# Tile loop of the first stage: the low half behind the moves, the halves' rows a step later, and a fourth half left to the projections

## What is computed

```python
def rmsnorm(x, g):
    y = x * lax.rsqrt(jnp.mean(x * x, axis=-1, keepdims=True) + 1e-6)
    return y * g

sh1, sc1, g1, sh2, sc2, g2 = split(silu(c) @ w_ada + b_ada, 6)   # per condition: prompt, sample
h = rmsnorm(x, norm_mix) * (1 + sc1) + sh1
qa, ka, va, fa, qb, kb, vb = split(h @ w_in)      # 8 forgetting heads, 8 band heads
logf = log_sigmoid(fa + b_f)                      # 8 gates per token
y = concat(head_rmsnorm(attend_a(qa, ka, va, cumsum(logf))),
           head_rmsnorm(attend_b(qb, kb, vb, rel_bias))) @ w_out
x = x + g1 * y
x = x + g2 * moe(rmsnorm(x, norm_ffn) * (1 + sc2) + sh2)          # 32 experts, 2 per token
out = rmsnorm(x, norm_final)
```

## Time and profile before

| | us |
|---|---|
| median of 3 runs | 1245.49 |
| lowest, highest | 1238.99, 1247.1 |
| time of the profiled execution | 1240.19 |
| its span | 1238.4 |
| PE busy in the span | 1100.7 (89%) |
| DVE, ACT, POOL busy | 491.6, 356.3, 366.4 |
| tile loop, first move to first projection | 34.66 to 90.00 |

### The profile page before, as it was taken

One profiled execution on the slowest core, in us unless ns is written; L12 is line 12 of the kernel. 1 busy time (PEld: TensorE's weight loads), 2 busy tenths in 40 slices (PEclk: granted clock), 3 DMA queues, 4 the chain that ended last, 5 costly groups with the idle time before them and its releaser, 6 DMA issues. The chain is left out here.

```text
span 1238.4 us, 20082 instructions
## 1 busy us (share of the span) xinstructions
PE 1100.7 (89%) x7180; PEld 767.1 (62%) x7180; DVE 491.6 (40%) x1307; ACT 356.3 (29%) x1130; POOL 366.4 (30%) x306
## 2 busy tenths in 40 slices
PE   5589999999999899999986899962999999989956
PEld 2348788888888788888875688851333333333322
DVE  0453344444444344453555267754111212111227
ACT  2643334434334334433454122210111111011102
POOL 1150633535353403113033144435222222121001
PEclk8799999999999999999999899975999999999978
DMA  9953323223141504021077511125999999999784
GB/s 382 404 196 110 96 69 108 93 64 101 62 118 34 166 1 120 14 72 45 1 221 212 188 69 69 69 103 215 398 374 373 413 414 393 406 368 422 281 306 158
DMA packets 86809, 238.63 MB, mean 193 GB/s; under 512 B 10456, under 2 KB 58024, under 8 KB 75952
## 3 DMA queue, kind: packets, MB, share of 16 engines
q1 hardware_dynamic: 68384, 132.01, 30.5%
q10 hardware_dynamic: 7344, 78.91, 15.8%
q0 software_dynamic: 10976, 26.32, 5.7%
HBM read 208.19 MB, written 38.45 MB: 199 GB/s over the span
## 5 line engine op out<-in xcount | busy, mean ns | idle before, releaser
L1987 PE MATMUL moe_gu_ps<-a_gu,moe_xT_sb 128*64 x416 | 185.1, 598 | 5.2 <-DMA b_gu<-in_w_gu 3.3
L942 PE MATMUL att_piece_ps<-hT_hi,w_hi 128*128 128x384 f32 (+1 forms) x528 | 184.4, 349 | 2.4 <-PEq L196 1.0
L1990 PE MATMUL moe_gu_ps<-b_gu,moe_xT_sb 128*64 128x512 f32 x416 | 185.1, 598 | 0.0
L942 PE MATMUL att_piece_ps<-hT_hi,w_lo 128*128 128x384 f32 (+1 forms) x528 | 172.7, 327 | 0.0
L942 PE MATMUL att_piece_ps<-hT_lo,w_hi 128*128 128x384 f32 (+1 forms) x528 | 172.5, 327 | 0.0
L1167 DVE COPY att_pT_sb<-att_pT_ps 128x512 f32<-128x512 f32 (+2 forms) x192 | 94.6, 520 | 133.4 <-PE att_pT_ps L1010 132.9
L1987 PEld LDWEIGHTS moe_gu_ps<-a_gu,moe_xT_sb 128*64 128x64 f32 x416 | 57.0, 138 | 125.7 <-issue 125.7
L1271 ACT ACTIVATE att_probs_sb<-att_probs_sb,att_nmax_sb 128x640 f32<-128x640 f32 (+5 forms) x144 | 101.4, 704 | 41.3 <-DVE att_nmax_sb L1153 40.6
L1289 ACT ACTIVATE keep_rows_all_sb<-att_o_ps,att_rden_sb 128x64 f32<-128x64 f32 x144 | 37.3, 310 | 246.8 <-PE att_o_ps L1031 246.8
L942 PEld LDWEIGHTS att_piece_ps<-hT_hi,w_hi 128*128 128x128 f32 x528 | 99.1, 188 | 11.1 <-issue 6.0
L1153 DVE CUSTOM_DVE_ANT_0 att_probs_sb<-att_s_ps,both_wide_sb 128x640 f32<-128x640 f32 (+5 forms) x144 | 95.3, 662 | 26.8 <-PE att_s_ps L998 15.0
(11 more groups left out here) (312 smaller groups left out, 1964.1 us busy)
## 6 DMA issues: line engine op xcount, KB each, us to landing
b_gu<-in_w_gu ACTq DMA_DIRECT2D x25, 2048.0 KB
b_dn<-in_w_dn ACTq DMA_DIRECT2D x25, 1024.0 KB
a_gu<-in_w_gu SPq DMA_DIRECT2D x10, 2048.0 KB
keep_rows_all_sb<-in_w_ada SPq DMA_DIRECT2D x9, 2048.0 KB, 11.2
att_w_raw_sb<-in_w_qkv SPq DMA_DIRECT2D x21, 512.0 KB, 3.7
a_dn<-in_w_dn SPq DMA_DIRECT2D x10, 1024.0 KB
w_out_parts<-keep_rows_all_sb SPq DMA_DIRECT2D x16, 512.0 KB, 4.8
in_w_ada_sb<-in_w_ada SPq DMA_DIRECT2D x3, 2048.0 KB, 16.6
```

The lines of the kernel that those rows point to most:

```text
L942: ins = pe.matmul(bank[:, 0:hi - lo], w[:, kind, kc, :], x[:, kc, lo:hi], start=(m == 0), stop=(m == 3 * NC - 1))
L1987: pe.matmul(gu_ps[p % 2][LANE[0], :], xT[:, c, LANE[0]], a_gu[:, bass.ds(slot, 1), c, :].rearrange("p a n -> p (a n)"), start=(c == 0), st ...
L1990: ins = pe.matmul(gu_ps[p % 2][LANE[1], :], xT[:, c, LANE[1]], b_gu[p % 3][:, c, :], start=(c == 0), stop=(c == NC - 1))
```

## The change

In the tile loop of `modulate_in`:

- Halves in the loop: four (4 to 7, at steps 2, 3, 4 and 6) in place of five (4 to 8, at steps 2 to 6). `EARLY` is 8, so four halves (8 to 11) are done in `attention`, after pieces 1, 3, 5 and 7. `W_HOME` follows.
- ScalarE copies a half's row one step after PE forms it; PE sums its columns two steps after, in place of one.
- VectorE does `lower(t - 1)` directly behind its move, ahead of `normalise` and `mean_square`, which change places.
- PE does the gate sum last in a step, behind the columns and the gate part.
- The last gate part is done in two pieces, columns of tiles 6 and 7 (256) and of tile 8 (64), each waiting for its own tiles' low half: 32 matmuls in place of 16.
- The two stores of the filler pattern are issued after all loads of the first stage (half 9 is the last), and SyncE does not wait for them there; VectorE waits for them in `attention`, before it overwrites part of their source.
- `X_FIRST`, which was `False`, is removed with its branches.

```diff
-EARLY = HALVES - 3
+EARLY = HALVES - 4
...
+    HALF_AT = {2: 4, 3: 5, 4: 6, 6: 7}
+
     def halves_at(t):
 
-        n = FIRST + t - 2
-        return [n] if FIRST <= n < min(EARLY, HALVES - HELD) else []
...
             if n == 6:
                 sp.wait_ge(xT_ready, 3)
                 sp.dma_start(raw, a["w_qkv"][0].rearrange("b p k n -> p b k n")).then_inc(raw_ld, 16)
-                sp.wait_ge(far_set, 1)
...
-        sp.wait_ge(far_stored, 32)
+        sp.wait_ge(far_set, 1)
+        entries = k["lists"].rearrange("(p n) c -> p (n c)", p=P)
+        sp.dma_start(entries[:, 0:D], far).then_inc(k["far_stored"], 16)
...
@@ scalar
-            for n in halves_at(t):
+            for n in halves_at(t - 1):
                 modulation_out(n)
...
@@ tensor, gate_part
-            pe.wait_ge(lo_done, (hi + P - 1) // P)
...
+            for n0, n1 in [(lo, min(hi, SEQ))] + [(SEQ, hi)] * (hi > SEQ):
+                pe.wait_ge(lo_done, (n1 + P - 1) // P)
+                for i, part in enumerate((h_hi, h_lo)):
+                    for kc in range(NC):
+                        ins = pe.matmul(f_ps[0:16, n0 - lo:n1 - lo], w_f_parts[:, kc, :], part[:, kc, n0:n1],
+                                        start=(i == 0 and kc == 0), stop=(i == 1 and kc == NC - 1))
...
@@ tensor, loop
-            if chunk_ending(t - 1) is not None:
-                gate_sum(chunk_ending(t - 1))
-            for n in halves_at(t - 1):
+            for n in halves_at(t - 2):
                 summed_columns(n)
             if chunk_ending(t) is not None:
                 gate_part(chunk_ending(t))
+            if chunk_ending(t - 1) is not None:
+                gate_sum(chunk_ending(t - 1))
...
@@ vector, loop
             move(t)
-            if t + ready < TILES:
-                if t + ready + 1 < TILES:
-                    mean_square(t + ready + 1)
-                normalise(t + ready)
             if t:
                 lower(t - 1)
+            if t + AHEAD < TILES:
+                normalise(t + AHEAD)
+            if t + AHEAD + 1 < TILES:
+                mean_square(t + AHEAD + 1)
...
@@ vector, attention, unit 0, step 1
                     if n == 0:
+                        dve.wait_ge(k["far_stored"], 32)
                         dve.wait_ge(pT_ready, turn["gates"] + 1)
```

More of the change, by code:

```diff
@@ L252, in modulate_in @@
     AHEAD = 3
-    X_FIRST = False
     w_ada = [k["rows_all"][:, 4 * j:4 * j + 4, :].rearrange("p t (a n) -> p (t a) n", a=2) for j in range(2)]
@@ L286, in modulate_in @@
     FIRST = 4
+    HALF_AT = {2: 4, 3: 5, 4: 6, 6: 7}
     def halves_at(t):
-        n = FIRST + t - 2
-        return [n] if FIRST <= n < min(EARLY, HALVES - HELD) else []
-    IN_LOOP = sum(len(halves_at(t)) for t in range(TILES))
+        return [HALF_AT[t]] if t in HALF_AT else []
     def chunk_ending(t):
@@ L325, in _ @@
             load_half(n)
-            if n == HELD and not X_FIRST:
+            if n == HELD:
                 for t in range(3, TILES):
@@ L404, in gate_rows_out @@
             act.activation(f_parts[:, 0:hi - lo], f_ps[:, 0:hi - lo], ACT.Copy).then_inc(f_moved, 1)
-        if X_FIRST:
-            for t in range(TILES):
-                square(t)
-            for n in range(FIRST):
-                modulation_out(n)
-        else:
-            for n in range(FIRST - 1):
-                modulation_out(n)
-            for t in range(AHEAD):
-                square(t)
-            modulation_out(FIRST - 1)
-            square(AHEAD)
+        for n in range(FIRST - 1):
+            modulation_out(n)
+        for t in range(AHEAD):
+            square(t)
+        modulation_out(FIRST - 1)
+        square(AHEAD)
         act.wait_ge(a1_done, 1)
@@ L421, in _ @@
             upper(t)
-            if t + AHEAD + 1 < TILES and not X_FIRST:
+            if t + AHEAD + 1 < TILES:
                 square(t + AHEAD + 1)
@@ L430, in _ @@
                 gate_rows_out(chunk_ending(t - 1))
-        for n in range(FIRST + IN_LOOP, EARLY):
+        for n in halves_at(TILES - 1):
             modulation_out(n)
@@ L464, in gate_part @@
             pe.wait_ge(wf_split, 2)
-            pe.wait_ge(lo_done, (hi + P - 1) // P)
             if c:
                 pe.wait_ge(z_done, c)
-            for i, part in enumerate((h_hi, h_lo)):
-                for kc in range(NC):
-                    ins = pe.matmul(f_ps[0:16, 0:hi - lo], w_f_parts[:, kc, :], part[:, kc, lo:hi],
-                                    start=(i == 0 and kc == 0), stop=(i == 1 and kc == NC - 1))
+            for n0, n1 in [(lo, min(hi, SEQ))] + [(SEQ, hi)] * (hi > SEQ):
[4 more added lines that the diff above has]
+                                        start=(i == 0 and kc == 0), stop=(i == 1 and kc == NC - 1))
             ins.then_inc(f_ready, 1)
@@ L481, in _ @@
         pe.wait_ge(silu_done, 1)
-        if X_FIRST:
-            transpose_x(0)
-            transpose_x(1)
         partial_rows(0)
         for n in range(1, FIRST):
-            if n == FIRST - 1 and not X_FIRST:
+            if n == FIRST - 1:
                 transpose_x(0)
@@ L504, in _ @@
                 gate_part(chunk_ending(t))
-        for n in halves_at(NT):
-            summed_columns(n)
-        for n in range(FIRST + IN_LOOP, EARLY):
-            partial_rows(n)
+            if chunk_ending(t - 1) is not None:
+                gate_sum(chunk_ending(t - 1))
+        for n in halves_at(TILES - 2) + halves_at(TILES - 1):
             summed_columns(n)
@@ L557, in logits @@
             dve.tensor_scalar(z[:, lo:end], f_ps[0:8, 0:end - lo], b_f[:, 0:1], None, ALU.add).then_inc(z_done, 1)
-        ready = TILES if X_FIRST else AHEAD
         mean_square(0)
-        for t in range(ready):
+        for t in range(AHEAD):
             if t + 1 < TILES:
```

30 lines of the change are left out of this document (10 added, 20 removed).

## The result

| | before | after |
|---|---|---|
| median (lowest to highest), 7 runs each | 1241.63 (1238.99 to 1247.54) | 1231.55 (1228.28 to 1234.56) |
| ratio, 95% interval | | 0.9904 (0.9881 to 0.9928) |
| profiled execution, span | 1240.19, 1238.4 | 1228.53, 1226.7 |
| first move, first projection | 34.66, 90.00 | 34.58, 73.87 |
| first transposes of probabilities, first values | 139.75, 145.04 | 126.50, 133.28 |

The change takes 10.1 us off the median; 10.4 was forecast. The same two kernels were compared twice more: 0.9923 (0.9890 to 0.9956) and 0.9933 (0.9913 to 0.9953), 9.0 us each. So the gain is 0.7 to 1.0%, small, and no comparison allows none.

A forecast was written before the change was run, and what follows sets the result against it. PE and ScalarE waiting for each other in the first stage's tile loop was taken as the bound. Stage end 90.0 to 75.5 (-14.5), +1.3 clock, +2.8 late half: net -10.4, from 1245.49 to 1235.1 us; 8 in 10 for 1230 to 1244.

The forecast's parts named there:

- the last step, where the sum is read: Reading of the whole-kernel forecast: about 1% (12.4 us) can be told from no change; within 1% given 0.66.
- the clock in the loop: Tile loop: one fall of PE's clock, 2.2 to 2.6 us, counted at half weight as 1.3 us.
- steps 1 and 2: Tile loop: later row copy cuts ScalarE's step from 6.7 to about 4.3 us; earlier low half starts tile 4's transposes about 43.65.
- step 3: Tile loop: PE becomes the longest chain, rows 1.92 us at the high clock, its list ending at 69.6 us.
- step 4: Last gate part cut in two: saves no wait, costs 3.6 us in place of about 2.5; stage ends at 75.5.
- step 5: First-stage loads: half 6 lands at 52.4 (wanted 52.5), half 7 at 61.3 (wanted 61.7); list stores cost nothing.
- third rival: Tile loop: PE stays at 1.2 GHz or a half is late; net -5 to -8 us, time 1239; chance 24%.
- step 6: Between projections: fourth late half adds 2.8 us; pair 1's V weights have 3.7 us of cover, so cost nothing.
- GpSimd last: First stage: GpSimd's three splits end at 74.6, costing nothing, or 2 us if weights land 3 us late; 1237; 10%.
- slower rival: Pair 1's V weights, behind the twelfth row and w_out in SyncE's queue, land 14 us later to break even; 3%.
- The sign: Behind the first stage: forecast wrong altogether if the stretches there change in length by more than 3 us.
- the likeliest one: Whole kernel: the forecast case, net -8 to -12.4 us, own range 1233 to 1238; chance 38%.

The follow-up runs named there:

- e3: The kernel before with only the row copy one step later and the columns two steps behind; ratio 1.0016.
- e4: The kernel before with only the low half directly behind the move; ratio 1.0009.
- e5: The kernel before with both loop edits (later row copy, low half behind the move), five halves in the loop, all else as before; ratio 1.0006.
- e2: The changed kernel with half 8 back in the tile loop at step 7, so three late halves; ratio 0.9945.
- e17: The changed kernel unaltered, compared with the kernel before a third time, on one chip with e16; ratio 0.9933.
- e1: The changed kernel unaltered, compared with the kernel before once more; ratio 0.9923.
- e9: The changed kernel with half 6 handled at step 5 in place of step 4; ratio 0.9907.
- e7: The changed kernel with the last gate part in one piece again; ratio 0.9928.
- e10: The changed kernel with spare matmuls, results never read, around the last gate part and sum and before the first transposes of probabilities; ratio 0.9869.
- e16: The same kernel as e10 run again, on one chip with the unaltered changed kernel; ratio 0.9872.

## Why the prediction came out as it did

- **What failed: the last step, where the sum is read.** "About 1% (12.4 us) is what a measurement of this kernel can tell from no change" made a forecast of -0.84% into one of no change that can be told, with 0.66 on it. The interval measured is 0.24% to either side, four times narrower, and the measured -0.96% stands clear of zero. In the sum itself three terms were off: the split gate part (3.6 against 2.5), the clock in the loop (1.3 against 0 in this profile) and the stretches behind the stage (nothing against +1.5). They and half a microsecond of PE's chain turn -10.4 into the -11.7 between the spans. That the medians differ by 10.1 is in part luck: terms of both signs, a clock that comes out differently in each execution, and a baseline of 3 runs.
- **The mutual wait, steps 1 and 2: right.** The transposes of tile 4 were put at 43.65 and stand at 43.49; ScalarE's step was put at 4.3 and is 4.0. The runs add what the prediction didn't say: neither edit alone, nor both with nothing else (e3, e4, e5), gains anything measurable; with the rest of the change, even five halves in the loop gain 0.5% (e2).
- **PE's chain, step 3: right within a microsecond.** Rows 5 to 7 ran at the high clock. The list was to end at 69.6; the last gate part starts at 69.11.
- **The split gate part, step 4: mis-sized.** Priced at 3.6 us with 1.1 for the 64-wide pieces; it took 2.5 (1.08, 1.10, 0.41, 0.40). The price came from tile 8's transposes, the upper end. The range had the lower one. With it the end of 75.5 is 74.4, measured 73.9.
- **The loads, step 5: right to 0.2 us, but its meaning was missed.** Half 6 lands at 31.75 + 20.6 = 52.4 (predicted 52.4), `raw` at 38.30 + 17.8 = 56.1 (56.2), half 7 at 48.68 + 12.4 = 61.1 (61.3). The loads of halves 6 and 7 in the trace of after:

```profile
L300 SPq DMA_DIRECT2D keep_rows_all_sb<-in_w_ada x1: 328/328/328, 31.7 to 31.7; - x1
...
DMA to landing us min/median/max: 20.6/20.6/20.6
```

```profile
L300 SPq DMA_DIRECT2D keep_rows_all_sb<-in_w_ada x1: 339/339/339, 48.7 to 48.7; - x1
...
DMA to landing us min/median/max: 12.4/12.4/12.4
```

  I treated these points as cover that might fail. They are the floor: with the mutual wait gone, half 7 lands at 60.5 to 61.9 in all profiles with this order of loads, whatever PE does, and what is left to vary is mostly the clock behind it, 12.8 to 17.5 us from the last rows to the first projection (61.1 to 73.9, 60.9 to 78.3).
- **The clock in the loop, 1.3 at half weight: mis-sized.** To the first projection it is 0 in the profiles of after and e17 and 4.5 in e1, three executions of one kernel, and 3.2 in e9. The third rival (a half late, the clock low) is therefore not another outcome but one that comes and goes between executions, with a half late (e1) or without (e9).
- **The fourth late half, step 6: right in the profile of after.** 2.88 us against 2.8; in e1 and e17 the same stretch is 4.5 longer than before (54.3 and 54.2 against 49.75), since the clock is low behind the start of the projections, a fall that the step had no term for. Its weights took 5.2 us to land against 5.5, and PE never waits for `w_lo` there. The slower rival did not appear.
- **GpSimd last: no.** Its three splits ended at 70.6. Beside VectorE's low halves the first two subtractions took 3.65 and 3.70, the third 2.70:

```profile
56.19 1.19 POOL L342 CAST w_hi<-in_x_sb 128x1024 fp32r<-128x1024 f32 x1 [2.18 <-DMA in_x_sb<-in_w_qkv]
57.46 3.65 POOL L344 TENSOR_TENSOR w_lo<-in_x_sb,w_hi 128x1024 fp32r<-128x1024 f32 x1
...
62.17 3.70 POOL L344 TENSOR_TENSOR w_lo<-in_x_sb,w_hi 128x1024 fp32r<-128x1024 f32 x1
...
67.93 2.70 POOL L344 TENSOR_TENSOR w_lo<-in_x_sb,w_hi 128x1024 fp32r<-128x1024 f32 x1
```

  against 4.03 beside a working VectorE and 2.35 beside an idle one. The Trainium skill (GPSIMD Engine Reference, 1. Specifications) says that the two engines share SBUF interfaces; the trace agrees, and in after the slowing did not reach the bound. In e7 it did, from the other side: there GpSimd's subtraction at 61.03 took 2.36, VectorE's low half beside it 2.68 in place of 1.20, and PE waited 2.46 us for the bias in place of 0.8. The rival priced GpSimd's delay alone.
- **Missed: what lies behind the stage.** The sign was a change in length "by more than 3 us", and it was not met: +1.5 at the first probabilities, then +1.4 and -1.4. The hole was in the profile of before, and I gave it no term because the clock had not fallen behind it. As 13 other profiles of unfilled kernels have the fall, kernels built on before among them, the +1.5 comes from that one profile of before and need not be a cost of the change.
- **The chances.** The sum gave -10.4; the three comparisons gave -10.1, -9.0 and -9.0, with 1231.55 inside the range and under the likeliest one's own (1233 to 1238). The distance of 3.6 us to the forecast of 1235.1 is that of the baseline: it was tied to a median of 1245.49 from 3 runs, and over 7 runs before's median is 1241.63, 3.9 lower. A gain just inside 1% was forecast and measured, and that isn't the same as no change, which is what the bound of 1% had been given for.

## What to carry to other kernels

When two engines wait for each other, look up what each would meet next once the wait is gone: here it was a queue of loads whose landing times were readable in the old trace. The two reorderings alone ran into it and showed no gain; with the rest of the change they gave 0.7 to 1.0%, and which of its parts are needed the runs don't separate. Price holes of a microsecond or two twice, once as they are and once with a low clock behind them, wherever they stand in the program and even if the profile at hand shows no fall. A median to which a forecast is tied should be of more than three runs, and a difference of a few microseconds between single profiles should be looked for in a second profile of the same kernel before it is explained.

## What the runs showed of the hardware

The granted clock fell or held behind holes of the same size. Behind the hole of 1.7 us for the first probabilities it held in the profile of before and fell in all 13 other profiles of unfilled kernels; behind the 2.4 us at 416 it fell in one profile of the changed kernel and held in another (e17). The Trainium skill (TensorE: Matmul & The Clock Gate, Part 1) says that the clock is low by default and that activity releases it; the trace agrees (after: 0.50 up to 48 us, with PE working without a hole from 43.5, then 0.98 and 1.00). Spare matmuls in the hole for the first probabilities kept the fall off in all six filled kernels (e10: 1.00 where after has 0.65 and 0.50); in e16, where 1.33 us of another hole stayed open, it fell. It also fell where PE had worked without a hole from 43.5 us on (e9, 1.00 up to 60 us, 0.93 and 0.50 in the two windows behind). Of a subtraction of GpSimd and a low half of VectorE that run at once, either can be the one slowed (after: 3.65 for GpSimd's at 57.46, with 1.21 for VectorE's; e7: 2.36 and 2.68). The landing of a 2 MB load in the full queue moved by 0.6 us when its issue came 1.7 us earlier (e1: 30.1 + 21.7 = 51.8, after: 52.4). Start to start, eight matmuls of 64 columns took 0.25 us (70.97 to 71.22) and eight of 256 columns 0.92: nearly by columns, while the prediction's upper end came from tile 8's 64-wide transposes, 8 in 0.82.
